# The fifth modulation vector moves from TensorE's column groups to VectorE, one unit behind each pooled addition of the third group

## The reference

```python
c_act = jax.nn.silu(c)
mod = c_act @ ada_w[i] + ada_b[i]                 # 1024 times 1024 x 6144
sh1, sc1, g1, sh2, sc2, g2 = jnp.split(mod, 6, axis=-1)
h = modulate(rmsnorm(x, norm_mix_g[i]), sh1, sc1)
x = x + g1[:, None, :] * pool_mixer(h, pool_w[j], pool_scale[j])
h = modulate(rmsnorm(x, norm_mlp_g[i]), sh2, sc2)
x = x + g2[:, None, :] * sq_relu_mlp(h, mlp_w1[i], mlp_w2[i])
```

## Time and profile before

| | |
|---|---|
| median of 3 runs | 2411.8 us (2408.84 to 2414.39) |
| the profiled execution | 2414.08 us, of which the span is 2412.3 us |
| PE busy | 2326.1 us, 96% of the span |
| DVE busy | 1759.1 us, 73% |
| ACT busy | 1143.6 us, 47% |
| POOL busy | 524.7 us, 22% |
| mean granted TensorE clock | 0.984 of full speed |

### The profile page before, as it was taken

One profiled execution on the slowest core, in us unless ns is written; L12 is line 12 of the kernel. 1 busy time (PEld: TensorE's weight loads), 2 busy tenths in 40 slices (PEclk: granted clock), 3 DMA queues, 4 the chain that ended last, 5 costly groups with the idle time before them and its releaser, 6 DMA issues.

```text
span 2412.3 us, 32666 instructions
## 1 busy us (share of the span) xinstructions
PE 2326.1 (96%) x11081; PEld 1906.9 (79%) x11081; DVE 1759.1 (73%) x2797; ACT 1143.6 (47%) x1982; POOL 524.7 (22%) x457
## 2 busy tenths in 40 slices
PE   5999999899999999999999999999999999998898
PEld 2678888788878788878888778888889887887777
DVE  7688778788786565277766877886678758998863
ACT  3455555444434223145555643443433337887741
POOL 0211001433232000201100233321030004566721
PEclk8999999999999999999999999999999999999999
DMA  9636656655425831325643754541346445436521
GB/s 362 245 113 234 220 203 226 231 165 166 136 97 141 275 96 50 142 97 179 210 163 134 262 174 151 165 135 36 140 142 170 161 140 134 105 88 161 151 71 70
DMA packets 272971, 382.16 MB, mean 158 GB/s; under 512 B 63665, under 2 KB 173489, under 8 KB 272818
## 3 DMA queue, kind: packets, MB, share of 16 engines
q1 hardware_dynamic: 272818, 380.21, 48.9%
HBM read 279.48 MB, written 106.70 MB: 160 GB/s over the span
## 4 chain that ended last, share of the span: by engine, by line
PE 83%; DVE 7%; issue 4%; ACT 2%; DMA 2%; POOL 1%; SPq 1%; DVEq 0%; POOLq 0%; ACTq 0%
PE banks L3048 22%; PE banks L3050 22%; PE banks L3049 22%; PE banks L3663 3%; PE banks L3643 3%; PE banks L3187 1%; PE banks L3623 1%; PE banks L3624 1%; PE banks L3066 1%; DVE X L2594 1%; DMA stage<-ada_w 1%; SPq L1410 1%; PE banks L3117 1%; PE banks L3606 1%; PE banks L3605 1%
## 5 line engine op out<-in xcount | busy, mean ns | idle before, releaser
L3048 PE MATMUL banks<-Hhi,Whi 128*128 128x512 f32 x1648 | 649.4, 394 | 19.7 <-DVE X L2594 12.0
L3050 PE MATMUL banks<-Hhi,Wlo 128*128 128x512 f32 x1648 | 644.4, 391 | 0.0
L3049 PE MATMUL banks<-Hlo,Whi 128*128 128x512 f32 x1648 | 644.2, 391 | 0.0
L3048 PEld LDWEIGHTS banks<-Hhi,Whi 128*128 128x128 f32 x1648 | 311.2, 189 | 92.3 <-issue 14.6
L3050 PEld LDWEIGHTS banks<-Hhi,Wlo 128*128 128x128 f32 x1648 | 311.0, 189 | 65.7
L3049 PEld LDWEIGHTS banks<-Hlo,Whi 128*128 128x128 f32 x1648 | 311.3, 189 | 63.6 <-issue 0.2
L3048 PE MATMUL banks<-T,Whi 128*128 128x512 f32 x720 | 283.0, 393 | 5.3 <-DVE Wlo L2513 4.3
L3049 PE MATMUL banks<-T,Whi 128*128 128x512 f32 x720 | 281.9, 392 | 0.0
L3050 PE MATMUL banks<-T,Wlo 128*128 128x512 f32 x720 | 281.7, 391 | 0.0
L1816 ACT ACTIVATE Whi<-stage 128x512 fp32r<-128x512 f32 (+2 forms) x186 | 107.7, 579 | 232.4 <-PE banks L3050 232.2
L2594 DVE SCALAR_TENSOR_TENSOR X<-banks,mod,X 128x512 f32<-128x512 f32 x180 | 134.2, 746 | 103.2 <-PE banks L3050 102.1
(11 more groups left out here) (288 smaller groups left out, 4346.0 us busy)
## 6 DMA issues: line engine op xcount, KB each, us to landing
stage<-w SPq DMA_DIRECT2D x58, 1024.0 KB, 6.7
stage<-hidden SPq DMA_DIRECT2D x224, 256.0 KB, 3.4
hidden<-slot SPq DMA_DIRECT2D x196, 256.0 KB, 2.1
stage<-ada_t SPq DMA_DIRECT2D x28, 1024.0 KB, 5.5
stage<-ada_w SPq DMA_DIRECT2D x20, 1024.0 KB, 8.2
x_saved<-X SPq DMA_DIRECT2D x32, 512.0 KB, 6.4
stage<-w_in SPq DMA_DIRECT2D x13, 1024.0 KB, 6.2
X<-x_saved SPq DMA_DIRECT2D x24, 512.0 KB, 4.9
```

The source lines that it names most:

```text
L3048: nc.tensor.matmul(out_bank, whi, xhi, start=start, stop=False, skip_group_check=onto)
L3049: nc.tensor.matmul(out_bank, whi, xlo, start=False, stop=False, skip_group_check=onto)
L3050: return nc.tensor.matmul(out_bank, wlo, xhi, start=False, stop=stop, skip_group_check=onto)
```

## The change

The fifth vector (`cc = 4`) leaves PE. Its four units, 16 to 19, are loaded from `ada_t` in place of `ada_w`, and DVE makes them with `ada`, one behind each of the tiles 8, 9, 10 and 11 of the pooled additions. `unit_done` is counted by DVE for these four. PE's program loses four `ada_rows` and one `turn_rows`, ACT's program loses one `copy_row`, and `rows` is no longer shared between the first and the fifth vector. `mods` adds the bias behind tile 15, where `first_mods(4, 4)` stood.

```diff
     def src_ada(l, cc, q):
-        if l == 0 and cc < 5:
+        if l == 0 and cc < 4:
             return ada_w.rearrange("(k p) n -> p k n", p=P)[:, 2 * q:2 * q + 2, cc * D:(cc + 1) * D]
         return ada_t[l].rearrange("(a p) k -> p a k", p=P)[:, cc * KT + 2 * q:cc * KT + 2 * q + 2, :]
...
                 act.wait_ge(row_ready, cc + 1)
                 act.wait_ge(unit_done, 4 * cc + 4)
-                if cc == 4:
-                    act.wait_ge(ada_sum, 1)
-                nc.scalar.activation(rows[:, cc % 4, :], row_bank(cc), ACT.Copy).then_inc(row_copied, 1)
+                nc.scalar.activation(rows[:, cc, :], row_bank(cc), ACT.Copy).then_inc(row_copied, 1)
...
                 squares_of(T, 2)
-                copy_row(4)
                 act.wait_ge(stage_in[20 % STAGES], 16 * (20 // STAGES + 1))
...
+                T.add(u=16)
                 add_pooled(0)
                 add_pooled(1)
-                add_pooled(2)
-                first_mods(3, 3)
+                for q in range(4):
+                    add_pooled(2, (q,))
+                    if q == 2:
+                        first_mods(3, 3)
+                    ada(T, 0, 4, q)
+                    T.add(u=1, ada=1)
                 add_pooled(3)
-                first_mods(4, 4)
+                T.add(mod=3)
+                dve.wait_ge(unit_done, 20)
+                mods(T, 0, 4)
+                T.add(u=-20, ada=-4, mod=-3)
...
                 turn_rows(3).then_inc(ada_sum, 1)
-                pe.wait_ge(mod_done, 2)
-                ada_rows(16)
-                pool_group(T, 2, (1, 2))
-                ada_rows(17)
-                pool_group(T, 2, (3,))
-                ada_rows(18)
-                pool_group(T, 3, (0,))
-                ada_rows(19)
-                pool_group(T, 3, (1, 2))
-                turn_rows(4).then_inc(ada_sum, 1)
-                pool_group(T, 3, (3,))
+                pool_group(T, 2, (1, 2, 3))
+                pool_group(T, 3)
                 pooled_seven(T, 0)
                 pooled_last(T, 0)
...
-        "ada_w": g["ada_w"][0][:, :5 * D],
+        "ada_w": g["ada_w"][0][:, :4 * D],
```

More of the change, by code:

```diff
@@ L2223, in ada @@
                 s = T.n["u"] % STAGES
-                if q == 0 and (l, cc) == (0, 3):
+                if q == 0 and (l, cc) == (0, 4):
                     dve.wait_ge(c_ready, 2)
@@ L2361, in pool, with add_pooled @@
                         chained(nc.vector.tensor_tensor(pg[:], mod[:, 0, 2 * KT:3 * KT], col("pool_scale"), ALU.mult))
+                T.add(u=16)
                 add_pooled(0)
                 add_pooled(1)
-                add_pooled(2)
-                first_mods(3, 3)
-                add_pooled(3)
-                first_mods(4, 4)
-            def add_pooled(j):
-                for i in range(4 * j, 4 * j + 4):
-                    hf, k = i % 4 // 2, KT - 2 - 2 * j + i % 2
+                for q in range(4):
[4 more added lines that the diff above has]
+                    T.add(u=1, ada=1)
+                add_pooled(3)
+                T.add(mod=3)
+                dve.wait_ge(unit_done, 20)
+                mods(T, 0, 4)
+                T.add(u=-20, ada=-4, mod=-3)
+            def add_pooled(j, tiles=range(4)):
+                for i in tiles:
+                    hf, k, i = i // 2, KT - 2 - 2 * j + i % 2, 4 * j + i
                     dve.wait_ge(d_ready, i + 1)
@@ L3128, in turn_rows @@
                 for j in range(KT // 2):
-                    ins = nc.tensor.matmul(mod_columns(cc)[:, j:KT:KT // 2], rows[:, cc % 4, j * P:(j + 1) * P], con("sel"),
+                    ins = nc.tensor.matmul(mod_columns(cc)[:, j:KT:KT // 2], rows[:, cc, j * P:(j + 1) * P], con("sel"),
                                            start=True, stop=True)
```

## The result

| kernel | median us | lowest to highest | runs | ratio to before, 95% |
|---|---|---|---|---|
| before | 2411.80 | 2408.55 to 2419.57 | 20 | |
| after | 2417.20 | 2412.98 to 2424.58 | 20 | 1.0024, 1.0017 to 1.0030 |

The change costs 5.4 us. The prediction was 2413.7, so its 1.9 us are 3.5 short. The time lies outside the forecast's own range (2412 to 2416) and inside the wide one, which takes in the rivals (2408.5 to 2418). The profiled execution took 2419.74 us with a span of 2417.9, 5.6 above the span before.

A forecast was written before the change was run, and what follows sets the result against it. PE was taken to bound the opening up to the first normed tile, the tail moving with it. Turns, PE's gap and low clock make that tile 1.9 us late: 2411.8 + 1.9 = 2413.7 us, range 2412 to 2416, wide 2408.5 to 2418.

The forecast's parts named there:

- its 1.9 us: Opening: the first normed tile starts at 100.3 in place of 98.42, and the end is as late; chance 0.50.
- the forecast's own range: Whole kernel: the main forecast's time lies between 2412 and 2416 us.
- the wide one: Whole kernel: range with the rivals, down to where 2 in 10 are left out, 2408.5 to 2418 us.
- the turns: Opening from 75.4 us: DVE's half units and POOL's sums exclude each other, 2.24 us a turn, 18.3 us in sum.
- PE's gap and the clock: PE idle from 89.1 to 93.65, 4.5 us; then low clock, a group of eight sums taking 1.57 us.
- The rival in which the clock holds: Sums behind PE's gap: turns, but full clock; first normed tile 0 to 0.6 late, 2412.1 us; chance 0.24.
- The rival in which the low clock reaches into the MLP: PE's first MLP products: low clock adds 3.5 us, 5.4 late in all, 2417.2 us; chance 0.14.
- ada_t in place of ada_w: Opening's loads: same bytes from another stride, priced at 0, within 1 us up or down.
- The step that fell short: From first normed tile to the end: the whole tail moves with that tile, so 1.9 us late there is 1.9 at the end.
- a rival's 2407 for the case without turns: Opening: half units and POOL's sums run side by side, inverse 4.75 earlier, 2407.1 us; chance 0.12.

The follow-up runs named there:

- a_psum: The changed kernel with the half units' second input taken from a PSUM bank in place of the SBUF row: 2411.1 us, ratio 0.9998.
- a_nosum: The changed kernel with POOL's sums of squares from tile 4 on cut to one column: 2411.4 us, ratio 1.0002.
- a_fill: The changed kernel with five 128x512 matmuls in PE's gap, into a bank nobody reads: 2413.2 us, ratio 1.0007.
- a_pe20: The changed kernel with 20 one-column matmuls ahead of PE's first work: 2417.8 us, ratio 1.0017.
- b_src: The kernel before with the narrower ada_w and units 16 to 19 loaded from ada_t, PE still multiplying them: 2411.1 us, ratio 0.9996.
- b_pe44: The kernel before with 44 one-column matmuls ahead of PE's first work: 2416.3 us, ratio 1.0015.
- a_ahead: The changed kernel with five matmuls in PE's gap, 15 small ones at its start, 12 DVE writes, each unit one tile earlier: 2411.4 us, ratio 0.9994.
- a_early: The changed kernel with ACT's squares of tiles 4 and 5 ahead of its copy of the fourth row: 2417.4 us, ratio 1.0022.
- b_pad: The kernel before with 21 one-column writes on DVE at its very start: 2410.0 us, ratio 0.9995.

## Why the prediction was right and where it was short

**What bounds, and the turns.** Right. A turn was put at 2.24 and is 2.21 (half units end at 75.46, 77.66, 79.87, 82.08 and so on); tile 12 at 17.45 behind tile 8 and is 17.29 behind. The order is strict turns, and a_psum and a_nosum show the cause.

**PE's gap and the clock.** Right in kind: 4.5 us forecast, 5.08 found; the end of the inverse 22.6 us behind tile 8, found 22.9. The first normed tile was put 1.9 late and is 2.3 late: the three groups of sums take 5.28 and not 4.7. The rival in which the clock holds falls with the window at 0.50, and a_fill shows the clock's share, 1.7 of 2.3. The rival in which the low clock reaches into the MLP gave 2417.2, the very time measured, and is still not what happened: it wanted the first product 5.4 late against tile 8, and it is 2.3 late (28.4 for 26.1), the clock being back at 101. In other executions it may reach there: in a_pe20, with the same opening, the clock is low until 104.2, 1.4 us behind the first product.

**ada_t in place of ada_w.** Put at 0 within 1 us: right, by b_src.

**The step that fell short** is the last one, which took the time lost at the first normed tile for the time lost at the end. I had written that the whole tail moves with it. It moves in place, but three further losses sit in it, X with 1.2 us, Y with 1.0 and Z with 1.2, and none comes from the opening's time. X and Z follow from DVE's program being 21 records longer, Y from where PE's packets of code meet SP's row of stores, which the 80 records fewer on PE moved.

The sum 2.3 + 1.2 + 1.0 + 1.2 = 5.7 stands against the 5.4 measured. That it comes so close is partly luck. The terms are of one execution (0.9 to 2.6 for the opening, 1.2 to 2.9 for X), and steps of up to 1.2 at other places have cancelled. The same sum for the other kernels of the table comes out right for b_pe44 (3.6 and 3.6) and within 0.5 for a_ahead, and 1.3 to 4.6 us above the measured in the ten others. The other places are as large: from 1660 to 1720 us b_src, b_pe44, a_nosum and a_early are 3.2 us shorter than before, whose clock is low for 13.7 us there and theirs for 6.8.

**Also wrong**, though it wasn't used: a rival's 2407 for the case without turns. Earlier work in the opening did not reach the end; a_psum had it and came out level. Right by luck is the wide range: it holds 2417.2 through the rivals on the clock, not through what X, Y and Z are.

What stays open: why DVE starts 0.36 us late at these records, and whether it does so every 128 where nothing hides it. It may be a fetch too, but no packet was tied to it; in after and b_pad the nearest of 8 KB begins 1.5 and 0.7 us behind the late start. Open too is why an issue of SP that meets a packet is long in this row and mostly not elsewhere.

## What to carry to other kernels

Work moved from PE to DVE under POOL costs twice: here 0.6 us for the turns at the port, and 1.7 more for the clock of the PE that is left waiting; five idle matmuls in the gap bought the second back. And where a kernel is tuned to the last 0.2%, adding or removing instructions moves later fetches of code against the transfers, and what comes of it can be larger than the edit's own effect: compare the same two products in both traces stretch by stretch, do not leave out what lies behind the last one, and pad the program before blaming the edit.

## What the runs showed of the hardware

- Code is fetched while PE runs: packets of 16 KB on queue 8, 86 in before, one for every 257 records of PE's program or so. In SP's row of stores the issue that meets one takes 1.2 to 2.2 us in place of 0.5 to 0.6 (before at 1816.7, after at 1802.1 and 1825.0, b_pe44 at 1795.9 and 1818.8). Elsewhere most are not longer: of the 19 issues of before in which such a packet begins, 14 take 0.32 to 0.43.
- 44 one-column matmuls where PE was idle made a kernel 0.15% slower (0.04 to 0.25), at a mean granted clock no lower than before's (0.9849 and 0.9843).
- DVE's 192nd, 320th or 448th record starts 0.36 us late where DVE is free: in b_pad, in the six kernels with 21 records more, in the three with 32.
- A packet of 8 KB of code that begins 2.0 us behind DVE's last instruction comes with 1.2 us more until the end (3.8 for 2.63) in five of six kernels, and with 0.5 in a_nosum.
- A half unit against a sum: 1.22 alone, 2.28 behind it, and 1.21 beside it with one input in PSUM.
- The clock was low near 90 to 100 us in every kernel here, but for 3.4 or 6.8 us where PE waited 1.8 us or less and for 10.2 or 13.7 behind a wait of 4.5 to 5.1; the one-column sums and the spread ran in it at 0.50.
